# A two-layer decoder trunk with product-key experts: last sum and norm read in PSUM, one-row look-up of expert numbers, expert batches placed by engine

## What is computed

```python
PEER_HEADS = 8; PEER_KEYS = 128; PEER_EXPERTS = 128 ** 2; PEER_TOPK = 16; TOKEN_CHUNK = 128

def _peer(h, wq, sub_keys, u, v):
    q = (hf @ wq).reshape(T, PEER_HEADS, 2, PEER_HALF)
    s_half = jnp.einsum('thpc,pnc->thpn', q, sub_keys)
    v_half, i_half = lax.top_k(s_half, PEER_TOPK)
    cand = (v_half[:, :, 0, :, None] + v_half[:, :, 1, None, :]).reshape(T, PEER_HEADS, 256)
    cand_idx = (i_half[:, :, 0, :, None] * PEER_KEYS + i_half[:, :, 1, None, :]).reshape(T, PEER_HEADS, 256)
    top_s, top_pos = lax.top_k(cand, PEER_TOPK)
    expert_idx = jnp.take_along_axis(cand_idx, top_pos, axis=-1)
    gate = jax.nn.softmax(top_s, axis=-1)
    def chunk(hc, ic, gc):                       # 128 tokens
        act = jax.nn.gelu(jnp.einsum('cd,chkd->chk', hc, u[ic]))
        return jnp.einsum('chk,chkd->cd', gc * act, v[ic])

def reference(x, mem, ...):
    for l in range(2):
        x = x + mixer(rmsnorm(x))
        x = x + cross_attention(rmsnorm(x), rmsnorm(mem))
        x = x + _peer(rmsnorm(x), ...)
    return rmsnorm(x, final_g)
```

## Time and profile before

| | us |
|---|---|
| median of the runs (3) | 1760.89 |
| lowest and highest | 1759.98, 1761.31 |
| the profiled execution | 1762.63 |
| its span in the trace | 1760.8 |

### The profile page before, as it was taken

The page is one execution under the profiler, slowest core; times in us unless marked ns, Lnnn a source line. Parts: engine busy times, 40 slices in busy tenths (PEclk is TensorE's granted clock), DMA queues, the critical chain, the costliest instruction groups (busy, mean ns, idle before and its releaser), DMA issues. The chain is left out here.

```text
span 1760.8 us, 22766 instructions
## 1 busy us (share of the span) xinstructions
PE 1338.8 (76%) x8310; PEld 686.1 (39%) x8310; DVE 1094.5 (62%) x2746; ACT 515.2 (29%) x1295; POOL 663.1 (38%) x1028
## 2 busy tenths in 40 slices
PE   8999886679999857667888766767888865565655
PEld 5856842245564523222354433233354531111111
DVE  5510588984333849779434757798444868964444
ACT  3411232262312222226332222225332323221112
POOL 0000234344333424435434434344433545565451
PEclk9999988799999978878989888778999977887778
DMA  9755599999999999999999999999999999999996
GB/s 387 293 169 182 209 421 421 414 394 422 411 421 421 420 410 405 421 396 414 422 421 422 421 421 420 422 386 421 421 421 421 421 418 400 407 420 422 421 421 272
DMA packets 95728, 689.00 MB, mean 391 GB/s; under 512 B 11008, under 2 KB 11136, under 8 KB 12288
## 3 DMA queue, kind: packets, MB, share of 16 engines
q0 software_dynamic: 73728, 536.90, 74.0%
q1 hardware_dynamic: 21888, 150.64, 21.3%
HBM read 685.40 MB, written 2.10 MB: 390 GB/s over the span
## 5 line engine op out<-in xcount | busy, mean ns | idle before, releaser
L521 POOL DMA_INDIRECT uv_rows<-uv_in,idx x512 | 504.0, 984 | 1055.5 <-PE acc_pe L1307 817.5
L1307 PE MATMUL acc_pe<-uv_rows,diag 64*64 64x512 f32 x4096 | 616.5, 731 | 322.7 <-ACT diag L1036 307.9
L566 DVE CUSTOM_DVE_ANT_0 uv_rows<-uv_rows,h_ps 128x1024 f32<-128x1024 f32 x512 | 606.7, 1218 | 232.4 <-DMA uv_rows<-uv_in,idx 220.6
L1307 PEld LDWEIGHTS acc_pe<-uv_rows,diag 64*64 64x64 f32 x4096 | 154.5, 153 | 693.1 <-ACT diag L1036 481.8
L1029 ACT ACTIVATE gelu_b<-act_b,h_scale 128x2 f32<-128x2 f32 x255 | 75.0, 294 | 744.0 <-DVE act_b L566 739.1
L1337 PEld LDWEIGHTS bank<-h_t,w_own 128*128 128x128 f32 x1504 | 171.0, 193 | 18.0 <-issue 18.0
L1361 PE MATMUL bank<-w_own,h_t 128*128 128x512 f32 x384 | 176.0, 612 | 2.3 <-ACTq L1077 2.2
L1337 PE MATMUL bank<-h_t,w_own 128*128 128x128 f32 x1504 | 175.1, 278 | 0.0
L515 POOL TENSOR_TENSOR diag<-ident_st,gate 128x64 f32<-128x64 f32 x512 | 159.0, 311 | 9.6
L1036 ACT ACTIVATE diag<-diag,gelu_b 128x64 f32<-128x64 f32 x510 | 149.6, 340 | 8.3
L1361 PEld LDWEIGHTS bank<-w_own,h_t 128*128 128x128 f32 x384 | 73.2, 196 | 107.8 <-issue 103.7
(11 more groups left out here) (208 smaller groups left out, 1170.5 us busy)
## 6 DMA issues: line engine op xcount, KB each, us to landing
w_own<-blocks_in SPq DMA_DIRECT2D x112, 1024.0 KB, 10.5
uv_rows<-blocks_in SPq DMA_DIRECT2D x24, 1024.0 KB, 10.4
uv_rows<-uv_in,idx POOLq DMA_INDIRECT x512, 15.4
xs<-x_in SPq DMA_DIRECT2D x2, 512.0 KB, 13.5
uv_rows<-mem_in SPq DMA_DIRECT2D x1, 1024.0 KB, 13.8
mem_gained<-uv_rows SPq DMA_DIRECT2D x1, 1024.0 KB, 14.1
area<-mem_gained SPq DMA_DIRECT2D x1, 1024.0 KB, 8.9
smalls<-smalls_in SPq DMA_DIRECT2D x1, 816.5 KB, 13.5
```

What stands on the lines that cost most here:

```text
L521: nc.gpsimd.indirect_dma_start(uv_rows[:, slot_of(k, earlier), :, :].rearrange("p a n -> p (a n)"), None, a["uv"], bass.IndirectOffsetOnAx ...
L566: v.tensor_tensor_reduce(u_row, u_row, h_ps[:, :], 1.0, 0.0, ALU.mult, ALU.add, act_b[:, k // B % AHEAD, k % B:k % B + 1]).then_inc(sems[" ...
L1307: mm = pe.matmul(acc_pe[c * HT:(c + 1) * HT, r * BLK:(r + 1) * BLK], diag[tok, slot_of(k), :], uv_rows[tok, slot_of(k), 1, c * BLK:(c + 1) ...
```

## The change

**The last sum and norm.** In the last stage acc_pe begins with the residual: two products of the identity and xs (tile 1) stand ahead of the first number. The halves of the products go elsewhere: row half r of the tokens now lands on partition half r, columns c in bank c, so that acc_pe has the layout of xs. (Before, and still in the other stages, partition half c and bank r.) The idle products are gone, experts_end is skipped, and the squares and the output's product read acc_pe. ScalarE waits for sums_done, which the last number's products raise, one for each bank. Behind its last diag ScalarE takes a root of a zero, whose result nobody uses.

```diff
                     def experts_end():
+                        if last:
+                            return
...
-                            rows = xs[:, D + c * BLK:D + (c + 1) * BLK]
-                            v.scalar_tensor_tensor(out=rows, in0=rows, scalar=st[:, 3:4], in1=final_gain[:, cols],
+                            v.scalar_tensor_tensor(out=xs[:, D + c * BLK:D + (c + 1) * BLK], in0=acc_pe[:, cols], scalar=st[:, 3:4], in1=final_gain[:, cols],
...
+                                s.activation(roots[:, 0:1], zero[:, 0:1], ACT.Sqrt)
                                 return
...
-                            act.wait_ge(sems["experts_added"], 2 * c + 2)
-                            s.activation(junk[:, c * BLK:(c + 1) * BLK], xs[:, D + c * BLK:D + (c + 1) * BLK],
+                            act.wait_ge(sems["sums_done"], c + 1)
+                            s.activation(junk[:, c * BLK:(c + 1) * BLK], acc_pe[:, c * BLK:(c + 1) * BLK],
...
-                            if last and k >= PAIRS - 3 * B and k % B == 0:
-                                for _ in range(3):
-                                    pe.matmul(bank[0][:, :], ident[:, :], mem_v[:, 0, 0:BLK], start=True, stop=True)
...
-                                    mm = pe.matmul(acc_pe[c * HT:(c + 1) * HT, r * BLK:(r + 1) * BLK],
+                                    y, x = (r, c) if last else (c, r)
+                                    mm = pe.matmul(acc_pe[y * HT:(y + 1) * HT, x * BLK:(x + 1) * BLK],
...
+                                if last and k == PAIRS - 1:
+                                    mm.then_inc(sems["sums_done"], 1)
+                            if not (last and k == PAIRS - 1):
+                                mm.then_inc(sems["slots_free"], 1)
...
+                        if last:
+
+                            for c in range(2):
+                                pe.matmul(acc_pe[:, c * BLK:(c + 1) * BLK], ident[:, :],
+                                          xs[:, D + c * BLK:D + (c + 1) * BLK], start=True, stop=False,
+                                          skip_group_check=True)
```

```diff
+                            step.mark(v.tensor_scalar(pos_q[:, :, :, 0], where, 4, None, ALU.logical_shift_right))
+                            step(v.tensor_scalar(pos_q[:, :, :, 1], where, 15, None, ALU.bitwise_and))
+                            step.mark(v.tensor_copy(pos_f, pos_q))
+                            step(v.tensor_scalar(half_f[:, :, 0, :], half_f[:, :, 0, :], float(PK), expert_base[:, :],
+                                                 ALU.mult, ALU.add))
...
+                            step(v.tensor_tensor(one_hot.rearrange("p (s i) -> p s i", i=TOPK),
...
+                        step(v.tensor_tensor(hot, hot, half_f.rearrange("p h e i -> p h (e i)").unsqueeze(
+                            2).to_broadcast([P, n, TOPK, 2 * TOPK]), ALU.mult))
+                        row = pos_f[:, :, 0:8, :].rearrange("p h k e -> p h (k e)")
+                        step(v.tensor_reduce(row, hot, AX.X, ALU.add))
+                        v.tensor_copy(idx[:, TOPK * heads[0]:TOPK * (heads[0] + n)].rearrange(
+                            "p (h k) -> p h k", h=n), row).then_inc(sems[signal], 1)
```

```diff
-TURNS = spread(PLAN, NB - 2)
-MEM_TURNS = spread(MEM_PLAN, NB - 2)
-LAST_TURNS = spread(LAST_PLAN, 21)
+BATCHES = {
...
+    None: {
+        "rank1": (0, 2, 1), "rank_more1": (1, 1, 0), "rank_pairs1": (1, 0, 1), "rank_pairs_more1": (1, 0, 0),
...
-                    n = turns.get(name, {}).get(step_name, 0)
+                    n = batches[step_name][ENGINES.index(name)] if step_name in batches else 0
```

More of the change, by code:

```diff
@@ L202 @@
+ENGINES = ("vector", "scalar", "tensor")
 TURN_PARTS = [6.25]
@@ L331, in stage @@
             plan = LAST_PLAN if last else FIRST_PLAN if first else PLAN if mem_layer is None else MEM_PLAN
-            turns = {} if first else LAST_TURNS if last else TURNS if mem_layer is None else MEM_TURNS
+            batches = {} if first else BATCHES[dense]
             if dense is not None:
@@ L931, in look_up @@
[L931 to L937 removed]
+                        q, n, h0 = heads[0] // 2, len(heads), heads[0] % 2
```

89 lines of the change are left out of this document (43 added, 46 removed), and 41 rows, old and new, of the table BATCHES.

## The result

The changed kernel took 1786.88 us (median of 4 runs, 1785.31 to 1788.13) against 1761.1 of the kernel before on the same chip: a ratio of 1.0143, with a 95% interval of 1.0126 to 1.0161. That is 25 us slower, where 1750.1 was forecast and the range ended at 1761.5. The profiled execution took 1785.31 us, with a span of 1783.3; line L605 is now the dot, L1356 the expert product, L1087 the diag and L560 the gather.

What follows compares the result with a forecast made beforehand. The prediction took the DMA stream of expert-row gathers as the bound. From 1760.89 us it took 0.8 (look-up), 3.5 (end) and 6.5 (places of batches), together 10.8, giving 1750.1, range 1741 to 1761.5.

Steps and rivals of the forecast that it cites:

- The look-up: VectorE's one-row look-up ahead of the first gather: 0.8 us earlier, bounds 0.5 to 1.0; the other sixteen counted at nothing.
- The end: From last diag to first output: idle products and adds gone, table loaded earlier; 3.5 us gained, bounds -2 and 4.2.
- Rival (c): TensorE stays at its low clock at the end: the tail gives -2 instead of 3.5, 1755.6; chance 0.09.
- The two products of the residual: Ahead of the last stage's first number on TensorE: hidden, so no cost; without cover 1.9 us once, in slots.
- Rival (d): Last stage: the two diagonal quarters, writing one bank, go one after the other; 1934 to 1947 us, chance 0.04.
- The places of the batches: Moving each engine's dots, diags and products between dense steps: 6.5 us gained, ends -5 and 15.
- the last stage can return to the stream's pace: Last stage: routing among 30 batches, not 22, lowers VectorE's share from 92% to 77%; 3 of 4.3 us gained.
- A lump of up to some 11 us is hidden: Routing between two dots: ten slots cover 24.9 us, a slot needs about 13; beyond some 11 a lump costs its excess.
- the order is changed by one to three batches here and there: Stages 1 to 3: lumps of 9 to 12 us, VectorE's total unchanged; 3.5 of 9.4 us of thin stretches gained.
- Rival (b): Stream dries at a stage's front, up to 5 us lost in the last: 1761.6, chance 0.16; sign: 1435 to 1467 under 390.
- The other four stretches: Thin stretches of the stream at 331 to 399, 683 to 775, 1143 to 1167, 1467 to 1551: near 418 GB/s forecast.
- Rival (a): The batches' placement returns nothing, lumps cost what the spread gains: 4.3 us gained in all, 1756.6; chance 0.19.

Runs made afterwards that it cites:

- e9: The kernel before with the one-row look-up alone: 1756.72 us, ratio 0.9973.
- e1: The changed kernel with the batches at their old, even places; the one-row look-up and new end stay: 1754.03 us, ratio 0.9952.
- e8: The changed kernel with the old places of the batches except in the last stage, which keeps the table: 1762.36 us, ratio 0.9995.
- e6: The changed kernel with the old places, but the last stage's routing spread evenly over 30 batches, not 21: 1754.34 us, ratio 0.9953.
- e14: The changed kernel with the old places, but TensorE two batches behind the others, not one: 1764.85 us, ratio 1.0006.
- e7: The changed kernel with the old places, but TensorE three batches behind the others, not one: 1825.42 us, ratio 1.0353.
- e4: The changed kernel, VectorE and ScalarE as in the table, TensorE one batch behind the later of the two: 1775.94 us, ratio 1.0068.
- e3: The changed kernel, VectorE as in the table, ScalarE at VectorE's places, TensorE one batch behind: 1788.12 us, ratio 1.0144.
- e12: The changed kernel with the old places, but two batches ahead of each stage's first step, not one: 1750.59 us, ratio 0.9938.

## Why the prediction was wrong, point by point

**What bounds the kernel** was read rightly: the stream of gathers does. The 27 us that the changed kernel lost up to its last dot went in stretches where gathers waited for slots, and the rest of the change lies at the end.

**The look-up** was mis-sized: 0.8 us forecast, 4.8 measured alone. The first gather came 1.24 us earlier, a little over the upper bound, but not all of that is left at the first dot (0.3 us earlier in the changed kernel; in e9 1.8 at the gather and 0.9 at the dot). The step that failed is "In the other sixteen look-ups the saving is as small ... and I count it at nothing". The shorter look-ups took 13.5 us of VectorE's work away, and in e9 the dots ran ahead by a little more in each stage. The prediction left what this frees where VectorE is packed to its term for the places; the look-up gave it without them.

**The end** was right: 3.5 forecast, 3.2 measured alone (1.1 to 5.5). In the trace 8.16 us became 3.63, against 8.2 and about 4 forecast; what the range kept for a low clock did not come. Rival (c) falls: the granted clock is 0.93 in the last stage of the changed kernel and 0.99 in e1, where it was 0.77.

**The two products of the residual** cost nothing that can be seen: in e1, which holds them, the last stage runs at 418 GB/s, where it was 416.

**Rival (d)** falls: the two diagonal quarters run side by side into one bank. Two numbers take 3.65 us, 1.83 each, as the forecast's "about 3.9" for two; one after the other would be 3.8 to 3.9 each. For products of two row halves that go to different partitions of a bank, the measurement goes against the rule that the prediction cited from the Trainium skill, "TensorEngine Tiling (Array Packing)", Gotcha 1 under Restrictions and Gotchas, and with the separate RAM of each bank and partition that it cited from the Trainium skill, "PSUM — Partial Sum Buffer", PSUM bank collisions raise a hardware error.

**The places of the batches** are where the prediction was wrong: a gain of 6.5 us forecast, with -5 as the worst; a loss of 31 alone and 34 with the rest measured. Three steps of it failed.
- That the last stage can return to the stream's pace because VectorE's share falls from 92% to 77% took one engine's share for the limit. A slot is held from the landing to the last product, and that path passes three engines; the table moved the places of ScalarE and TensorE more than VectorE's. With the table in the last stage VectorE's share does fall, and the stream is at 398 in place of 422 (e8). An even spread over 30 batches lowers VectorE's share too, from 86% to 83% of the stretch 1435 to 1551, and returns it to 420, with no gain shown in the time (e6).
- "A lump of up to some 11 us is hidden": the allowance itself did not fail, since with the even places of e1 gathers waited up to 18.3 us with stages 1 to 3 at 417 to 419 GB/s. But it was held only against the routing on VectorE. TensorE's and ScalarE's own lumps were not added up, though the order shows them: xq in stage 3 was named, "TensorE four batches behind VectorE", and got no price. It was the hole of 22 us at 333 GB/s shown above. By the prediction's own estimates, the 13 us that a slot needs plus up to 20 for four batches are more than 24.9.
- For stages 1 to 3, "the order is changed by one to three batches here and there" set the price by the size of the moves. e14 and e7 show that TensorE one batch later everywhere costs 10 us in all and two batches later 71.

**Rival (b)** was right as a mechanism and at half its size for the last stage (up to 5 us; e8 lost 7.6, 2.6 of it in the first 26 us), but it was asked at one place only. In the changed kernel the same question has the same answer at the front of stage 2, where a gather waited 26 us. Its sign, 1435 to 1467 under 390, has to move with the stage, whose first dot came 23.3 us later:

```profile
1435.00:1467.00 32.00, 16.41 (x74) 5.65 (x68) 20.85 (x68) 5.25 (x15) 11.85 (x19) 0.73 0.98 400
1458.00:1490.00 32.00, 24.51 (x96) 7.23 (x98) 28.96 (x78) 8.97 (x24) 15.33 (x21) 0.84 0.93 363
```

The other four stretches stand at 402, 422, 421 and 388 in the changed kernel, where about 418 was forecast: holes went, and others came elsewhere. **Rival (a)**, no gain, was too mild, and no case held a loss by lumps on all engines together: the lower bound of -5 was taken from the one front.

What stays open is why e4 costs half of what e3 costs with as many pauses (the 13 us lie in stage 1: 19.3 against 3.5), how much the places level with or ahead of the other engines cost in the table, and why e12 is as fast as it is.

## What to carry to other kernels

Where a ring of buffers feeds a stream, ask of another order how long a buffer is held from landing to release, over every engine on the way: walk through the order of the last engine, add up what stands between two releases, and hold it against what the ring covers. That finds the holes; it did not give their price here, and a long wait can be free while other transfers keep the DMA engines busy. An even interleaving with one batch of lag was hard to beat here: none cost 281 us more, two 10, three 71, and a table with a place for each engine 34. Taking work off VectorE paid 4.8 us in all, of which the use ahead of the first gather made some 0.3 to 0.9 at the first dot; the later ones, counted at nothing, made the rest.

## What the runs showed of the hardware

- Products of two 64 x 64 quarters on the diagonal, into one bank and different partitions, overlap: 3.65 us for two numbers, against 1.95 for all four quarters at once and some 7.7 if they had gone one after the other (an estimate from the earlier trace rows).
- TensorE doing the same columns in two quarters at a time was busier (224 of 301 us in e1's last stage, 171 of 301 before) and was granted 0.99 of its full clock, 2.4 GHz, there in place of 0.77, with no idle products.
